# First half of the experts' up products as four column strips of 32 tokens

## The reference

```python
x_sorted = tok[token_of]                                    # tokens sorted by expert, 4 experts each
gu = lax.ragged_dot(x_sorted, w_up, group_sizes) + b_up[e_sorted]     # 1024 -> 2048 = [g | u]
g, u = gu[:, :1024], gu[:, 1024:]
g = jnp.minimum(g, 7.0); u = jnp.clip(u, -7.0, 7.0)
act = (u + 1.0) * (g * jax.nn.sigmoid(1.702 * g))
out = lax.ragged_dot(act, w_down, group_sizes) + b_down[e_sorted]     # 1024 -> 1024
```

## Time and profile before

| | |
|---|---|
| time, median of 3 runs | 2461.74 us (2461.18 to 2462.36) |
| span of the profiled execution, first to last instruction | 2460.5 us |
| TensorE busy | 2221.8 us (90%) |
| weight loads busy (beside the matmuls) | 1532.9 us (62%) |
| VectorE, ScalarE, GpSimd busy | 58%, 39%, 5% |
| share of TensorE in the chain that ended last | 85% |
| experts' stage | from 1080 to about 2320 us |

### The profile page before, as it was taken

How to read it: one execution, slowest core, us unless ns; L and a number is a source line. 1 busy time by engine, 2 the same in 40 slices (tenths; PEclk the granted TensorE clock), 3 DMA queues, 4 the chain that set the end, 5 groups by cost and what they waited for, 6 DMA issues and landing times.

```text
span 2460.5 us, 27486 instructions
## 1 busy us (share of the span) xinstructions
PE 2221.8 (90%) x8811; PEld 1532.9 (62%) x8876; DVE 1421.8 (58%) x1720; ACT 959.0 (39%) x1177; POOL 120.9 (5%) x141
## 2 busy tenths in 40 slices
PE   4998897979779999849999999999999999999858
PEld 3776776867545554525767667676666766667623
DVE  4666666856521110326767777676776767767542
ACT  3444244243110110114545555455554555545513
POOL 0000010100100000030000000000000000000020
PEclk9999898989889999869999999999999999999969
DMA  3225121212042220439999999999999999999540
GB/s 101 69 60 196 52 69 52 67 41 62 1 145 77 68 69 19 156 107 393 351 351 368 340 359 352 349 363 343 360 350 352 361 340 364 350 352 360 211 148 34
DMA packets 307103, 526.58 MB, mean 214 GB/s; under 512 B 17638, under 2 KB 125750, under 8 KB 307062
## 3 DMA queue, kind: packets, MB, share of 16 engines
q1 hardware_dynamic: 291776, 480.67, 56.7%
q0 software_dynamic: 7424, 25.19, 2.8%
q10 hardware_dynamic: 7862, 20.19, 2.1%
HBM read 496.50 MB, written 29.49 MB: 214 GB/s over the span
## 4 chain that ended last, share of the span: by engine, by line
PE 85%; DVE 7%; issue 2%; ACT 2%; DMA 2%; POOL 1%; ACTq 0%; DVEq 0%; POOLq 0%; SPq 0%
PE psum L1474 80%; PE psum L1746 1%; PE psum L1752 1%; DVE arena L1075 1%; PE psum L1594 1%; PE psum L1481 1%; POOL slots_dram L608 1%; PE psum L1641 1%; DMA arena<-y_dram,rows_u 1%; DMA arena<-in_lambda_k 0%; DVE residual L1445 0%; ACT w_hi L690 0%; ACT arena L802 0%; DVE arena L982 0%; DMA arena<-in_w_in 0%
## 5 line engine op out<-in xcount | busy, mean ns | idle before, releaser
L1474 PE MATMUL psum<-arena 128*128 128x512 f32 (+7 forms) x2384 | 865.5, 528 | 43.2 <-DVE arena L1269 13.4
L1474 PEld LDWEIGHTS psum<-arena 128*128 128x128 f32 (+1 forms) x2384 | 410.5, 196 | 467.9 <-issue 418.5
L1474 PE MATMUL psum<-h_hi,w_hi 128*128 128x512 f32 x1664 | 666.0, 400 | 7.4 <-DVE h_lo L1380 5.1
L1474 PE MATMUL psum<-h_hi,w_lo 128*128 128x512 f32 x1664 | 650.4, 391 | 0.0
L1474 PE MATMUL psum<-h_lo,w_hi 128*128 128x512 f32 x1664 | 650.0, 391 | 0.0
L1380 DVE TENSOR_TENSOR h_lo<-arena,h_hi 128x1024 fp32r<-128x1024 f32 x512 | 600.8, 1219 | 33.2 <-ACT h_hi L886 20.4
L886 ACT ACTIVATE h_hi<-arena 128x1024 fp32r<-128x1024 f32 x512 | 520.3, 1052 | 83.2 <-PE psum L1474 75.0
L1474 PEld LDWEIGHTS psum<-h_hi,w_hi 128*128 128x128 f32 x1664 | 314.0, 189 | 81.1 <-issue 16.5
L1474 PEld LDWEIGHTS psum<-h_hi,w_lo 128*128 128x128 f32 x1664 | 313.4, 188 | 66.8
L1474 PEld LDWEIGHTS psum<-h_lo,w_hi 128*128 128x128 f32 x1664 | 314.0, 189 | 65.4 <-issue 3.8
L954 DVE TENSOR_TENSOR w_lo<-arena,w_hi 128x1024 fp32r<-128x1024 f32 x80 | 100.4, 1257 | 131.4 <-ACT w_hi L690 131.1
(11 more groups left out here) (249 smaller groups left out, 1449.4 us busy)
## 6 DMA issues: line engine op xcount, KB each, us to landing
arena<-in_w_up SPq DMA_DIRECT2D x512, 512.0 KB, 6.6
arena<-in_w_down SPq DMA_DIRECT2D x128, 1024.0 KB, 9.1
arena<-in_w_in SPq DMA_DIRECT2D x80, 512.0 KB, 3.9
y_dram<-arena ACTq DMA_DIRECT2D x32, 512.0 KB, 5.3
arena<-in_w_ssd_branch SPq DMA_DIRECT2D x8, 1024.0 KB, 5.6
y_dram<-arena SPq DMA_DIRECT2D x1, 7680.0 KB, 23.0
arena<-in_w_attn_branch SPq DMA_DIRECT2D x8, 512.0 KB, 3.8
arena<-in_w_out SPq DMA_DIRECT2D x2, 2048.0 KB, 13.2
```

What stands on the lines that cost most here:

```text
L1474: return pe.matmul(o, l, r, start=start, stop=stop)
```

## The change

The 16 plain float32 products of `up(b, 0)` are each divided into four. A strip takes 32 of the 128 tokens: the stationary operand is 128x32, the moving operand is the same 128x512 of weights each time, and the output is the strip's own 32 partitions of the bank, which puts the strips into four different column groups of TensorE's array. 16 products of two passes become 64 products of two passes in each block. `up(b, 1)`, `down` and everything else stay. The semaphore of a unit, `up_used`, is now raised by the last strip of the unit's last product.

```diff
+STRIP = 32
...
                         for j in range(2):
                             for u in range(2):
-                                ins = mm(bank(u), xgT[:, 2 * c + j, :], w_unit_up[0][c][:, j, u, :],
-                                         c == 0 and j == 0, False)
+                                for s in range(0, P, STRIP):
+                                    ins = mm(bank(u)[s:s + STRIP], xgT[:, 2 * c + j, s:s + STRIP],
+                                             w_unit_up[0][c][:, j, u, :], c == 0 and j == 0, False)
                         ins.then_inc(up_used, 1)
```

## The result

The changed kernel takes 2471.03 us (median of 5 runs, 2469.33 to 2473.29) against 2461.74 us before: 1.004 times as long, 95% interval 1.0027 to 1.0052. That is slower by 9.3 us, where 16.6 us were forecast; it lies inside the forecast's own range of 2468 to 2495 us, and well inside the stated one of 2465 to 2925 us. The span of the profiled execution is 2469.3 us against 2460.5 us. `mm`'s line is now L1475, and every later line is one further.

The account below looks back on a forecast made before the run. TensorE was taken to bound each expert round; 0.23 us for layout plus 0.29 us for further tiles made 0.52 us a round, times 32 16.6 us, giving 2478.3 us; own range 2468 to 2495, stated range 2465 to 2925 us.

Parts of the forecast that it names:

- TensorE sets the round, 32 times: Expert rounds: TensorE bounds each 38.6 us round, so time added to its part is added 32 times.
- A strip's pass streams as long as a full one: `up(b, 0)`: a pass with 32 columns of weights still takes 0.429 us, with 128 passes instead of 32.
- Column strips overlap as the two row halves of the scores do: `up(b, 0)`: four column strips run at once, so streaming stays at 32 x 0.429 us a round.
- Further tiles cost 9 ns a pass, 0.29 us a round: `up(b, 0)`: three more tiles add 9 ns to each of 32 passes; bounds nothing and 0.64 us a round.
- The two changes of layout cost 0.23 us a round: Into and out of the strips: 0.09 + 0.03 + 0.09 + 0.02 us a round, from 0.21 to 0.40.
- Pairs: Rival in `up(b, 0)`: strip passes start in program order, two at a time; 447 us more, 2909 us; chance 0.18.
- the strict order of matmuls: Trainium skill's rule that matmuls start and end in program order, whatever their tile; gives the Pairs rival's time, 2909 us.
- Exposed loads: Rival in `up(b, 0)`: strips overlap, but weight loads don't hide under running passes; 44 to 126 us more; chance 0.11.
- No overlap: Rival in `up(b, 0)`: strips go one behind another, eight slots instead of two; 1327 us more, 3789 us; chance 0.08.
- not slower: Rival: strips and full array follow without a gap and no pass gets longer; 0 us, 2461.7 us; chance 0.05.

Follow-up runs that it names:

- `one_group`: Changed kernel, but after a full-array first step all four strips put their output into partitions 0 to 31, one column group: 3622.88 us, ratio 1.4714.
- The experiments with one, two and four ways in and out: Changed kernel with half of the 16 products in strips, switching between strips and full array once, twice or four times a round: 2471.96, 2481.54, 2503.51 us.
- `strip_outer`: Changed kernel with the strips as the outer loop of a unit, 8 passes in a row for one group: 2976.67 us, 1.2091 times before.
- `alt_steps`: Changed kernel with step j = 0 of every unit in strips of 32, j = 1 in the full array: 2503.51 us, ratio 1.0165.

## Why the prediction was right, point by point

**TensorE sets the round, 32 times.** Right: the round grew by 0.28 us, the span by 8.8 us, and in all kernels here the time follows the first piece of the round.

**A strip's pass streams as long as a full one.** Right: 0.429 us in every strip kernel, and `one_group` shows 112 of them in a line.

**Column strips overlap as the two row halves of the scores do.** Right, and this was the step on which 400 us hung: four at a time, all 32 slots. But the reason was given too freely. "Different parts of the array take their work independently" holds as far as a group's queue does not fill, and it fills with 4 passes. The change puts 2 in a row into a group; with 8 the same sentence would have been wrong by 500 us. That the change stayed under 4 was luck: the prediction didn't ask how many passes in a row go to one group. The scores' rows, with 2 passes in a row, could not have shown the difference.

**Further tiles cost 9 ns a pass, 0.29 us a round.** Wrong: nothing. The four start within 0.02 us of each other, and this shows once a round, not 32 times; after the first, distances are 0.429 us as in the full array. This is the term that was mis-sized, and with it the sum: 0.28 instead of 0.52 us a round, 9.3 instead of 16.6 us.

**The two changes of layout cost 0.23 us a round.** Right: 0.245, with 0.095 in (predicted 0.09), 0.024 of exposed load (0.03), 0.111 out (0.09, without the last strip's later start of 0.02) and 0.015 (0.02). The experiments with one, two and four ways in and out show that they are the cost. The four strips' first loads go side by side (0.02, not 0.11).

**Pairs; the strict order of matmuls.** Out: the first passes of four strips start together although a second pass stands before three of them. The rule of the Trainium skill ("TensorE: Matmul & The Clock Gate", "The mechanism") that matmuls start strictly in program order does not hold for these; in `strip_outer` a pass of strip 1 starts ahead of three of strip 0 that stand before it. What is in order is the leaving of the program, by the counts above.

**Exposed loads.** Out: the loads of the following passes start while the running passes go through the same rows, and the distances stay at 0.429 us. In this trace the sentence of the Trainium skill (same page and section) that loads overlap only where the row group differs doesn't hold either; the section also lets a load go ahead into a background weight buffer, and no run here tells whether that is what happens.

**No overlap, not slower.** Out; 0.245 us a round is above the 0.154 us at which "not slower" would have decided.

What stays open: 0.03 of the 0.28 us a round lie outside the changed piece, mostly in the one behind it (`up(b, 1)`, 10.92 us instead of 10.89), for which no experiment was made. It isn't a fixed price of the strips, since in `alt_steps` that piece is 10.89 us again. Why a way in or out takes 0.09 us was not taken apart either.

## What to carry to other kernels

Dividing a full-width product into column strips gained nothing here, since each strip streams the whole moving operand again; if the strips go to different groups of 32 partitions, it costs only the change of layout, here about 0.1 us each way and the first load behind it, so switch seldom and never inside a loop of products. When narrow products are to share the array, change the group after at most 4 passes (2 plain fp32 products), better after each product: the same products in another order cost 506 us here. Products of a single pass (fp32r, bf16) were not tried in strips. Before trusting an overlap seen elsewhere in a trace, compare how many instructions in a row go to one part of the array there and in the new code.

## What the runs showed of the hardware

- Plain fp32 passes in four column groups run fully side by side, though each streams the same 128 rows of the moving operand: 0.429 us for one, two or four at a time.
- Matmuls of different column groups don't start in program order; a group takes up to 4 passes, the running one included, before what follows in the program has to wait (32, 44, 36 and 68 slots counted, as this rule gives). With plain fp32, 4 passes are 2 products, and which of the two is the limit was not separated.
- A change between full array and strips is 0.09 to 0.11 us each way, and the first load behind it is exposed: 0.024 us for 32 columns, 0.104 us for 128.
